# Closing a layer norm half of the tokens at a time, in a two-block float32r kernel on one core

## The chip, the core and the metric

The kernel runs on one core of a Trainium2 chip. The metric is the device time of one execution in microseconds (us). Before the change it is 2527.17 us, the median of 3 runs (2527.03 to 2527.21).

TensorE (PE) multiplies: an instruction keeps a 128x128 stationary operand, which a weight load (PEld) puts in place, and streams a moving operand of up to 512 columns past it. ScalarE (ACT), VectorE (DVE) and GpSimd (POOL) do the elementwise work, and SyncE (SP) issues the loads from memory. Each engine works through its own row of instructions in order and waits on semaphores for the others.

## What is computed

Two blocks of two layers each, on 256 tokens of 2048 features:

```python
# first block: a state-space mixer, then sparse attention, each followed by a layer norm
h = ssd_mixer(x, ...)                       # ... @ ssd_w_out: 4096 -> 2048
x = layer_norm(4**0.25 * x + h, ln_g[0], ln_b[0])
h = dsa_mixer(x, ...)                       # x @ dsa_w_in at its start, ... @ dsa_w_out at its end
x = layer_norm(4**0.25 * x + h, ln_g[1], ln_b[1])
# second block: gated MLP with token mixing, then stick-breaking attention, each behind an RMS norm
hn = rms_norm_2(h, norm_g[0]); h = h + gmlp_branch(hn, ...)      # hn @ a_w_in at its start
...
```

`layer_norm` takes mean and variance of a token over its 2048 features, so no part of its output for a token exists before the last feature of that token is there. Different tokens do not depend on each other in it.

## The kernel before, in words

All weights stream through the core once. Activations lie transposed: features on the 128 partitions, 256 tokens along the columns. `AA[:, k, 0, :]` is the leading (float32r) part of feature tile k (of 16), `AA[:, k, 1, :]` the rest, and each product is made of three float32r matmuls: leading x leading, leading weight x rest, rest of the weight x leading.

A **unit** is one load of 128x1024 weights (512 KB). SP fetches it into one of four `RAW` buffers. ACT copies it to a slot as the leading part (`e.copy`, L1038), DVE writes the rest (L1448, `RAW - leading`), and PE runs the unit's matmuls (L597). There are three slots `W0` to `W2`, and in some stretches one or two more (`WY24`, `WY28`, `Wx7`). A slot is refilled when the unit in it is done. A block is all units of one output tile: `("o1", i)` and `("o2", i)` are the output projections, in tiles of 4, 4, 4, 2, 1 and 1 feature tiles (`OUT_COLS`); `("cq", 0)` is the first block behind the first layer norm, `("v5", 0)` the first behind the second. Each has 8 units of 24 matmuls of 256 columns (`cq`) or of 12 matmuls of 512 columns (`v5`, where activations are the stationary operand and weights the moving one). `("o1", 5)` and `("o2", 5)` have 4 units of 24 matmuls of 256 columns.

The order of the work is written out by hand in `walk`: `unit(u)` lets each engine append its part of a unit, and `tick()` advances every side task, written as a generator, to its next `yield`.

At the end of a layer norm s (1 or 2), the last block's result is added to `RES` (DVE L1689), squared (ACT L1147) and summed over the features by matmuls with ones on PE (`ln_sums`). Then `ln_end` makes mean `MU` and 1/sqrt(variance) `RS` (ACT L1158 and L1160, DVE L1700 to L1707), POOL subtracts the mean from 15 feature tiles, and `norm_in` makes the first tiles of `AA` in `CHUNKS` of 1, 1, 2, 2, ... feature tiles: DVE multiplies by `RS` (L1723), ACT applies gain and bias (L1177, L1180) and copies to the leading part (L1188), DVE writes the rest (L1452). PE waits before the first matmul on each chunk:

```python
if (name == "cq" or (name, i) in (("v5", 0),)) and k in [c[0] for c in CHUNKS]:
    e.wait_ge(*on("at" + ("1" if name == "cq" else "2"), k))
```

`rms4` takes the RMS norm's sum of squares of the second layer norm's output: DVE applies gain and bias in place, POOL squares four tiles at a time and folds them, PE sums them with ones. Its result scales the output of `v5` (`ev_v5`).

Of the kernel before, what the change touches and what calls it, by code (L numbers as in the profile page):

```python
# [11 lines left out]
P = 128  # L12
T = 256
# [14 lines left out]
CHUNKS = ((0, 1), (1, 1)) + tuple((k, 2) for k in range(2, 16, 2))  # L28


class Plan:


    def __init__(self, A):
# [51 lines left out]
        self.before = {b: self.order[i - 2] if i > 1 else None for i, b in enumerate(self.order)}  # L86
        self.slots()

# [24 lines left out]
    def slots(self):  # L113
# [9 lines left out]
        for u in range(len(self.units)):  # L123
            for name, (a, z) in extra.items():
                if u == a:
                    free.append((name, None))
            alive = 3 + sum(a <= u < z for a, z in extra.values())
            free = [x for x in free if x[0] not in extra or u < extra[x[0]][1]]
            while ready < min(u + alive, len(self.units)) and free:
                self.slot[ready], self.prior[ready] = free.pop(0)  # L130
                self.turn.setdefault(u, []).append(ready)
                ready += 1
            s = self.slot[u]
            free.append((s, u))
            self.slot_end[s] = u
# [26 lines left out]
def program(nc, A, out, at, bank, counting):  # L162
# [84 lines left out]
    def region(specs):  # L247
# [16 lines left out]
        ("MU2", [P, T], F), ("RS2", [P, T], F)])  # L264
    (CK, CQ, QKB, VVB, SG, OT, KI, WT, SC, MA, TRL, PXB, PT, M8, MXB) = region([
# [8 lines left out]
        ("VS5", [P, 2, 8], F), ("VR5", [P, 2], F), ("GB5", [P, 2, 16], F)])  # L274
    (_, SQ6, GH6) = region([("keep6", [P, 16, T], F), ("SQ6", [P, 4, T], F), ("GH6", [P, 4, T], F)])
# [11 lines left out]
    SQ4, GH4 = U5, Z5  # L287
    VA = V5[:, 0, 0:5 * T].rearrange("p (a n) -> p a n", a=5)
# [5 lines left out]
    def pair_of(u):  # L294
        s = plan.slot[u]
        if s in (0, 1, 2):
            w = (W3M if units[u][0][0] == "o4" else W3)[s]
            return w[:, 0:UW], w[:, UW:2 * UW]
# [45 lines left out]
    def walk(unit, go):  # L344
# [30 lines left out]

        def later(n, *do):
# [50 lines left out]
        for i in range(1, 6):  # L427
            run(("o2", i), ("ln_block", 2, i))
        drain()
        start("ln_end", 2)  # L430
        tick()
        start("norm_in", 2)
        start("rms4", late=1)
        tick()
        for j in range(8):
            run(("v5", j), later(9 if j == 0 else 1 if j == 1 else 0, "ev_v5", j))
# [43 lines left out]
    def sync_program():  # L480
# [16 lines left out]
        def unit(u):  # L497
            for v in plan.turn.get(u, ()):
# [93 lines left out]
    def tensor_program():  # L592
# [21 lines left out]
        def unit(u):  # L614
# [3 lines left out]
            if u == us[0] and plan.before[b]:  # L618
                e.wait_ge(*on("g_read", plan.before[b]))
            e.wait_ge(*on("rest", u))  # L620
# [32 lines left out]
            for j, k in enumerate(kts):  # L653
# [6 lines left out]
                if (name == "cq" or (name, i) in (("v5", 0),)) and k in [c[0] for c in CHUNKS]:  # L660
                    e.wait_ge(*on("at" + ("1" if name == "cq" else "2"), k))
                if (name, i) == ("q7", 0) and k in [c[0] for c in OUT_COLS]:
                    e.wait_ge(*on("at3", k))
                if name in ("v5", "v7", "o4"):
                    for t in range(2):
# [12 lines left out]
            last.then_inc(*up(unit_done, "unit", u))  # L678
# [97 lines left out]
        def ln_sums(s, i):  # L776
# [14 lines left out]
            for f, v in enumerate(vals):  # L791
                ones_sum(M[:, b1, 0:T], v, i == 0 and f == 0, i == 5 and f == n - 1)
            e.wait_ge(*on("ln_sq", s, i))
            for f, v in enumerate(sqs):
                last = ones_sum(M[:, b2, 0:T], v, i == 0 and f == 0, i == 5 and f == n - 1)
            last.then_inc(*up(pe_made, "ln_m", s, i))
            if i == 5:
                ring.extend((b1, b2))
# [100 lines left out]
        def rms4():  # L899
            for i, k in enumerate(range(0, 16, 4)):  # L900
                yield
                yield
                yield
                ones_of("r5", i, SQ4[:, 0, :], ("r5_f", i), i == 3)
            yield
            yield
            yield
# [100 lines left out]
        def set8():  # L1008
# [5 lines left out]
                        ln_block=ln_block, set3=set3, ev_cq=ev_cq, ev_ms=ev_ms, index=index, attend=attend,  # L1014
# [4 lines left out]
    def scalar_program():  # L1019
        e = nc.scalar  # L1020

        def unit(u):
            for v in plan.turn.get(u, ()):
# [9 lines left out]
                elif plan.slot[v] == "y5":  # L1033
                    e.wait_ge(*on("unit", plan.blocks["o2", 5][-1]))
                elif plan.slot[v] == "x7":
# [101 lines left out]
        def ln_square(s, i):  # L1137
# [3 lines left out]
            if i == 5:  # L1141
                e.wait_ge(*on("eps"))
                e.activation(TB[:, :], eps6[:, :], ACT.Sqrt).then_inc(*up(act_made, "tb", s))
# [10 lines left out]
        def ln_end(s):  # L1154
            PV, RS = (PV2[:, :], RS2[:, :]) if s == 1 else (VA[:, 0, :], VA[:, 2, :])
            b1 = bank.get(("ln", s, 0), 0)
            e.wait_ge(*on("ln_m", s, 5))
            e.activation(PV, M[:, b1, 0:T], ACT.Square, scale=1.0 / DM).then_inc(*up(act_made, "ln_mm", s))  # L1158
            e.wait_ge(*on("read", "ln", s, 1))
# [1207 lines left out]
```

## Time and profile before

| | |
|---|---|
| median of 3 runs | 2527.17 us |
| profiled execution, its own time | 2528.34 us |
| its span from first to last instruction | 2527.1 us |
| PE busy | 2467.4 us (98%) |
| DVE, ACT, POOL busy | 64%, 49%, 5% |
| stretch from the end of ("o1", 5) to the end of ("cq", 0) | 37.99 us |
| stretch from the end of ("o2", 5) to the end of ("v5", 0) | 50.00 us |

Busy time of PE says how long an instruction was in it, its span says when the last result was there. The chain of work that ended last runs through PE for 90% of the span, so time is lost or won where PE stands still, where its clock is low, or where it has more to do.

### The profile page before, as it was taken

How to read it: one execution, taken by the hardware profiler on the slowest of the kernel's cores; microseconds unless marked ns; L12 is line 12 of the kernel's file. 1: busy time of each engine (PE TensorE's matmuls, PEld its weight loads, DVE VectorE, ACT ScalarE, POOL GpSimd, SP SyncE). 2: the span in 40 equal slices, each digit the busy share in tenths (PEclk: the TensorE clock that was granted, in tenths of full speed). 3: DMA queues.
4: the chain of work that ended last, by engine and by line, in shares of the span. 5: the costliest groups of instructions: out<-in, count | busy, mean ns of one | idle time of the engine just before them, and what ended most of it. 6: DMA issues, size and time to landing. Idle time of an engine off the chain costs nothing.

```text
span 2527.1 us, 45040 instructions
## 1 busy us (share of the span) xinstructions
PE 2467.4 (98%) x19470; PEld 2359.9 (93%) x19470; DVE 1609.6 (64%) x2120; ACT 1236.7 (49%) x1375; POOL 118.8 (5%) x96
## 2 busy tenths in 40 slices
PE   8999999999989999999979999999999999999998
PEld 8999999999979999999957889999999999899987
DVE  5778888866577776666475455665655555555556
ACT  3445665653455565643344444544544444454453
POOL 0001000100020000000050000000000000000002
PEclk9999999999999999999989999999999999999999
DMA  6766666555646555445635666666655665756645
GB/s 186 224 197 183 209 182 185 179 181 179 189 130 186 155 167 152 150 166 183 185 110 172 186 188 187 193 192 184 186 189 192 192 195 165 225 164 175 187 155 170
DMA packets 276232, 453.21 MB, mean 179 GB/s; under 512 B 18540, under 2 KB 82114, under 8 KB 274882
## 3 DMA queue, kind: packets, MB, share of 16 engines
q1 hardware_dynamic: 276033, 450.33, 59.1%
q8 instruction: 153, 2.51, 0.4%
q14 instruction: 46, 0.37, 0.0%
HBM read 445.89 MB, written 4.26 MB: 178 GB/s over the span
## 4 chain that ended last, share of the span: by engine, by line
PE 90%; DVE 5%; DMA 2%; ACT 1%; issue 1%; SPq 0%; POOL 0%; ACTq 0%; DVEq 0%; POOLq 0%
PE G L597 84%; PE M L597 6%; DVE W L1448 2%; PE M L610 1%; DMA h_scratch<-HT 1%; ACT W L1038 1%; DVE RES L1723 0%; DMA RAW<-in_b_w_in 0%; DVE AA L1452 0%; DMA CSB<-cs_scratch 0%; DMA WS<-in_a_w_s 0%; DVE WY L1448 0%; DVE BT L1487 0%; DMA XS<-in_x 0%; DMA RAW<-in_ssd_w_in 0%
## 5 line engine op out<-in xcount | busy, mean ns | idle before, releaser
L1448 DVE TENSOR_TENSOR W<-RAW,W 128x1024 fp32r<-128x1024 f32 (+1 forms) x632 | 783.6, 1242 | 589.9 <-ACT W L1038 588.2
L1038 ACT CAST W<-RAW 128x1024 fp32r<-128x1024 f32 (+1 forms) x632 | 659.1, 1048 | 738.3 <-PE G L597 708.9
L597 PE MATMUL G<-AA,W 128*128 128x256 f32 x8100 | 972.7, 279 | 18.8 <-DVE AA L1452 10.7
L597 PEld LDWEIGHTS G<-AA,W 128*128 128x128 f32 x8100 | 945.3, 189 | 27.3 <-issue 11.0
L597 PE MATMUL G<-YY,W 128*128 128x256 f32 x4608 | 534.8, 277 | 1.5 <-DVE W L1448 1.5
L597 PEld LDWEIGHTS G<-YY,W 128*128 128x128 f32 x4608 | 528.1, 188 | 4.2 <-DVE W L1448 2.4
L597 PE MATMUL G<-AA,WY 128*128 128x256 f32 x2508 | 305.8, 278 | 0.0
L597 PEld LDWEIGHTS G<-AA,WY 128*128 128x128 f32 x2508 | 293.8, 188 | 2.5 <-issue 2.2
L597 PE MATMUL G<-W,AA 128*128 128x512 f32 x864 | 216.6, 408 | 19.2 <-DVE AA L1452 15.7
L597 PEld LDWEIGHTS G<-W,AA 128*128 128x128 f32 x864 | 167.7, 195 | 62.8 <-issue 11.2
L1448 DVE TENSOR_TENSOR WY<-RAW,WY 128x1024 fp32r<-128x1024 f32 (+1 forms) x128 | 161.0, 1259 | 90.6 <-ACT WY L1038 90.5
L1038 ACT CAST WY<-RAW 128x1024 fp32r<-128x1024 f32 (+1 forms) x128 | 132.9, 1043 | 112.0 <-PE G L597 109.4
L597 PE MATMUL G<-AA,Wx 128*128 128x256 f32 x528 | 65.7, 281 | 0.0
L597 PEld LDWEIGHTS G<-AA,Wx 128*128 128x128 f32 x528 | 63.4, 192 | 0.0
L597 PE MATMUL G<-CQ,W 128*128 128x256 f32 x456 | 54.4, 278 | 0.0
L597 PEld LDWEIGHTS G<-CQ,W 128*128 128x128 f32 x456 | 52.9, 188 | 0.4 <-issue 0.3
L1268 ACT ACTIVATE PXB<-PXB,MXB 128x128 f32<-128x128 f32 x64 | 28.5, 447 | 50.2 <-DVE MXB L1906 50.1
L1038 ACT CAST Wx<-RAW 128x1024 fp32r<-128x1024 f32 x30 | 31.5, 1050 | 36.5 <-PE G L597 36.2
L1091 ACT ACTIVATE E<-E 128x1536 f32<-128x1536 f32 x16 | 23.8, 1489 | 49.7 <-DVE E L1542 49.7
L597 PE MATMUL G<-WY,AA 128*128 128x512 f32 x192 | 47.7, 396 | 0.0
L1448 DVE TENSOR_TENSOR Wx<-RAW,Wx 128x1024 fp32r<-128x1024 f32 x30 | 36.7, 1222 | 14.4 <-ACT Wx L1038 14.4
L597 PEld LDWEIGHTS G<-WY,AA 128*128 128x128 f32 x192 | 36.1, 188 | 8.9
(317 smaller groups left out, 1918.2 us busy)
## 6 DMA issues: line engine op xcount, KB each, us to landing
RAW<-in_a_w_in SPq DMA_DIRECT2D x192, 512.0 KB, 3.8
RAW<-in_ssd_w_in SPq DMA_DIRECT2D x160, 512.0 KB, 4.4
RAW<-in_b_w_in SPq DMA_DIRECT2D x128, 512.0 KB, 4.1
RAW<-in_dsa_w_in SPq DMA_DIRECT2D x72, 512.0 KB, 3.7
RAW<-in_ssd_w_out SPq DMA_DIRECT2D x64, 512.0 KB, 4.6
RAW<-in_dsa_w_out SPq DMA_DIRECT2D x64, 512.0 KB, 3.8
RAW<-in_a_w_out SPq DMA_DIRECT2D x64, 512.0 KB, 3.9
RAW<-in_b_w_out SPq DMA_DIRECT2D x32, 512.0 KB, 3.7
```

The costliest lines, as they stand in the source:

```text
L597: return e.matmul(o, l, r, start=start, stop=stop, skip_group_check=True)
L610: return e.transpose(o, i, idn)
L1038: e.copy(wh[:, 0:n], RAW[:, v % NR, 0:n]).then_inc(*up(cast_done, "cast", v))
L1091: e.activation(ev, ev, ACT.Exp).then_inc(*up(act_made, "ee", g, i))
L1268: e.activation(PX[:, a:z], PX[:, a:z], ACT.Exp, bias=MX[:, 2 + t:3 + t], accum_out=MX[:, 4 + t:5 + t]).then_inc(*up(act_made, "pe", j, h))
L1448: e.tensor_tensor(wl[:, 0:n], RAW[:, v % NR, 0:n], wh[:, 0:n].bitcast(F), ALU.subtract).then_inc(*up(rest_done, "rest", v))
```

## The change

- `("o1", 5)`, `("o2", 5)` and the first four units of `("cq", 0)` and `("v5", 0)` are done for tokens 0 to 127 and then for tokens 128 to 255. A matmul of 256 columns in `o1`, `o2` and `cq` becomes two of 128 columns. In `v5`, where the tokens are the stationary operand, the same 12 matmuls of 512 columns are only put in another order.
- `ln_close` takes the place of `ln_end`, `norm_in` and the last `ln_block`: add, square, sum, mean, root, mean subtraction, gain and both parts of `AA`, once for each half of the tokens, in five `PARTS` of 2, 2, 4, 4, 4 feature tiles.
- Four more weight slots (`WA0` to `WA3`) from the 15th unit of `("o1", 1)` to the end of `("cq", 0)`, and three (`WB0` to `WB2`) from `("o2", 1)` to the end of `("v5", 0)`.
- The squares of `rms4` move from POOL to ACT, alternate between two buffers, and `ev_v5` of block 0 starts behind the fifth unit of `("v5", 1)`.

```diff
+HALF = 128
+PARTS = ((0, 2), (2, 2), (4, 4), (8, 4), (12, 4))
+HALVED = (("o1", 5), ("cq", 0), ("o2", 5), ("v5", 0))
...
+        for b in self.order:
+            us = self.blocks[b]
+            n = 4 if b in HALVED else 0
+            self.steps += [(u, h) for h in range(2) for u in us[:n]] + [(u, None) for u in us[n:]]
...
+        for i in range(4):
+            extra[f"a{i}"] = (self.blocks["o1", 1][14], first["ms", 0])
+        for i in range(3):
+            extra[f"b{i}"] = (first["o2", 1], first["v5", 1])
...
+        def twice(b, *tasks):
+            us = plan.blocks[b]
+            for h in range(2):
+                for u in us[:4]:
+                    unit(u, h)
+                    if u == us[3] and h == 0:
+                        for t in tasks:
+                            start(*t[:-1], late=t[-1])
+                    tick()
+            for u in us[4:]:
+                unit(u)
+                tick()
...
-        for i in range(2, 6):
+        for i in range(2, 5):
             run(("o1", i), ("ln_block", 1, i))
-        drain()
-        start("ln_end", 1)
-        tick()
-        start("norm_in", 1)
-        tick()
-        run(("cq", 0))
+        twice(("o1", 5), ("ln_close", 1, 0))
+        twice(("cq", 0))
...
+        twice(("o2", 5), ("ln_close", 2, 0))
+        twice(("v5", 0), ("rms4", 2))
...
                     for f in range(width // P):
-                        o = G[:, half + f // 2, (f % 2) * T:(f % 2 + 1) * T]
+                        a, z = (0, T) if part is None else (HALF * part, HALF * part + HALF)
+                        o = G[:, half + f // 2, (f % 2) * T + a:(f % 2) * T + z]
...
-                        mm(o, h, X[:, k, 0, :], k == 0 and f % 2 == 0, False)
-                        mm(o, h, X[:, k, 1, :], False, False)
-                        last = mm(o, l, X[:, k, 0, :], False, k == nk - 1)
+                        mm(o, h, X[:, k, 0, a:z], k == 0 and first, False)
+                        mm(o, h, X[:, k, 1, a:z], False, False)
+                        last = mm(o, l, X[:, k, 0, a:z], False, k == nk - 1)
...
+            total(1)
+            normal(0, 4)
+            tails(0, 3)
+            yield
+            tails(0, 4)
+            scale(1)
+            yield
+            first_three(1)
```

On PE, at the close of the first layer norm (the one of `("o1", 5)` and `("cq", 0)`; `YY` is the projection's input, `RES_87,ones` and `SQ_89,ones` are the sums), the row before is:

```order
L597 MATMUL G<-YY,W_50 128x256 x24
L597 MATMUL M<-RES_87,ones 128x256
L597 MATMUL M<-SQ_89,ones 128x256
L597 MATMUL G<-YY,W_52 128x256 x24
L597 MATMUL M<-RES_87,ones 128x256
L597 MATMUL M<-SQ_89,ones 128x256
L597 MATMUL G<-AA,W_54 128x256 x24
L597 MATMUL G<-AA,W_50 128x256 x24
L597 MATMUL G<-AA,W_52 128x256 x24
```

and with the change, at the same place:

```order
L644 MATMUL G<-YY,WA_95 128x128 x24
L644 MATMUL G<-YY,W_50 128x128 x24
L644 MATMUL M<-RES_87,ones 128x128
L644 MATMUL M<-SQ_89,ones 128x128
L644 MATMUL G<-YY,WA_93 128x128 x24
L644 MATMUL G<-YY,WA_94 128x128 x24
L644 MATMUL G<-YY,WA_95 128x128 x24
L644 MATMUL G<-AA,WA_96 128x128 x24
L644 MATMUL M<-RES_87,ones 128x128
L644 MATMUL M<-SQ_89,ones 128x128
L644 MATMUL G<-AA,W_52 128x128 x24
L644 MATMUL G<-AA,W_54 128x128 x24
```

The sums of the first half now stand behind the first unit of the second half, with three more half units of `o1` behind them, and the sums of the second half stand behind the first half unit of `cq`. Every unit here counts 24 matmuls for 128 columns and comes twice.

On DVE, for the second half of the same layer norm, the change puts the work on the second half (L1815, L1824) between that on the first half (L1843, L1561) and the rests of the weights (L1557):

```order
L1557 TENSOR_TENSOR WA_93<-RAW,WA_93 128x1024
L1843 TENSOR_TENSOR RES_87<-RES_87,RS_92 128x4x128
L1561 TENSOR_TENSOR AA<-RES_87,AA 128x4x128
L1557 TENSOR_TENSOR WA_94<-RAW,WA_94 128x1024
L1815 TENSOR_TENSOR RES_87<-RES_87,G 128x128
L1843 TENSOR_TENSOR RES_87<-RES_87,RS_92 128x4x128
L1561 TENSOR_TENSOR AA<-RES_87,AA 128x4x128
L1557 TENSOR_TENSOR WA_95<-RAW,WA_95 128x1024
L1561 TENSOR_TENSOR AA<-RES_87,AA 128x4x128
L1824 SCALAR_TENSOR_TENSOR RS_92<-M,PV_88 128x128
```

Before, the whole row of the norm's end stood together and the weights came behind it:

```order
L1689 TENSOR_TENSOR RES_87<-RES_87,G 128x256
L1700 SCALAR_TENSOR_TENSOR RS_92<-M,PV_88 128x256
L1702 TENSOR_SCALAR MU_91<-M 128x256
L1705 TENSOR_TENSOR RES_87<-RES_87,MU_91 128x256
L1707 RECIPROCAL RS_92<-RS_92 128x256
L1723 TENSOR_TENSOR RES_87<-RES_87,RS_92 128x256
```

The addition for the second half (L1815) is the instruction for which PE's second pair of sums waits, and it stands behind two rests of weights.

## Rows read from the trace of the kernel before

**Rows 1.** The page: span, busy time of each engine.

```profile
span 2527.1 us, 45040 instructions
PE 2467.4 (98%) x19470; PEld 2359.9 (93%) x19470; DVE 1609.6 (64%) x2120; ACT 1236.7 (49%) x1375; POOL 118.8 (5%) x96
```

**Rows 2.** PE's waits, 675 to 760 us, then 1250 to 1360 us: total, times, longest.

```profile
PE G L597 <- DVE AA L1452: 10.7, 5, 6.5
PE M L597 <- DVE RES L1689: 0.5, 1, 0.5
...
PE G L597 <- DVE AA L1452: 15.7, 6, 6.5
PE G L597 <- ACT V L1315: 3.5, 1, 3.5
```

**Rows 3.** Busy time by stretch: length, each engine, granted clock, DMA share, GB/s.

```profile
697.91:735.90 37.99, 26.79 (x198) 25.50 (x199) 28.26 (x32) 22.00 (x35) 16.09 (x18) 0.87 0.32 93
...
1272.30:1322.30 50.00, 33.81 (x106) 25.23 (x106) 40.76 (x45) 23.54 (x36) 29.93 (x23) 0.80 0.32 94
1322.30:1349.33 27.03, 23.48 (x103) 18.69 (x102) 17.36 (x17) 12.40 (x14) 8.74 (x5) 1.00 0.63 176
```

**Rows 4.** Timeline, first two units of cq: start, length, engine, instruction, [idle before].

```profile
706.06 5.46 PE L597 MATMUL G<-AA,W 128*128 128x256 f32 x24 [6.50 <-DVE AA L1452]
...
712.01 3.01 PE L597 MATMUL G<-AA,W 128*128 128x256 f32 x24 [0.50 <-DVE AA L1452]
```

**Rows 5.** Timeline, five of the eight units of v5.

```profile
1280.46 5.22 PE L597 MATMUL G<-W,AA 128*128 128x512 f32 x12 [6.50 <-DVE AA L1452]
...
1288.09 4.58 PE L597 MATMUL G<-W,AA 128*128 128x512 f32 x12 [2.41 <-DVE AA L1452]
...
1295.73 4.48 PE L597 MATMUL G<-W,AA 128*128 128x512 f32 x12 [3.06 <-DVE AA L1452]
...
1303.96 3.04 PE L597 MATMUL G<-W,AA 128*128 128x512 f32 x12 [0.52 <-DVE AA L1452]
...
1313.23 5.46 PE L597 MATMUL G<-W,AA 128*128 128x512 f32 x12 [2.60 <-DVE AA L1452]
```

**Rows 6.** 256 columns by stretch, 512 columns by stretch, loads by form, narrow rows of timelines.

```profile
575.00:600.00 25.00, 25.00 (x223) 25.00 (x223) 12.58 (x11) 9.49 (x9) 0.00 (x0) 1.00 0.63 195
...
1400.00:1425.00 25.00, 25.00 (x109) 20.06 (x108) 12.26 (x13) 10.51 (x11) 0.00 (x0) 1.00 0.66 189
...
L597 PEld LDWEIGHTS G<-AA,W 128*128 128x128 f32 x8100 | 945.3, 189 | 27.3 <-issue 11.0 <-DVE W L1448 7.5 <-DVE AA L1452 6.9
...
L597 PEld LDWEIGHTS M<-E,XD 128*64 128x64 f32 x256 | 16.1, 136 | 8.3
...
1523.88 0.60 PE L597 MATMUL M<-WR,V 128*128 128x128 f32 x4
...
1523.77 0.52 PEld L597 LDWEIGHTS M<-WR,V 128*128 128x128 f32 x4
...
61.64 0.13 PEld L610 LDWEIGHTS M<-ident,SZ 64*128 64x128 f32 x1
61.70 0.14 PEld L610 LDWEIGHTS M<-ident,YT 64*128 64x128 f32 x1
```

**Rows 7.** Timeline of the first norm's end: root, mean, and one later chunk's work.

```profile
700.84 15.13 POOL L2284 TENSOR_TENSOR RES<-RES,MU 128x256 f32<-128x256 f32 x15 [150.33 <-DVE MU L1702]
701.14 1.74 DVE L1707 RECIPROCAL RS<-RS 128x256 f32<-128x256 f32 x1
...
720.71 1.09 ACT L1177 ACTIVATE RES<-RES,VC 128x256 f32<-128x256 f32 x2
720.84 1.23 DVE L1448 TENSOR_TENSOR W<-RAW,W 128x1024 fp32r<-128x1024 f32 x1 [1.98 <-ACT W L1038]
721.83 0.62 ACT L1188 CAST AA<-RES 128x512 fp32r<-128x512 f32 x1
721.98 0.68 DVE L1723 TENSOR_TENSOR RES<-RES,RS 128x512 f32<-128x512 f32 x1
```

More of the change, by code:

```diff
@@ L264, in program @@
         ("MU2", [P, T], F), ("RS2", [P, T], F)])
+    after = [s_at + 4 * (16 * T + T + 4 * T + 2 * T + T + T)]
+    WA = []
+    for i in range(4):
+        after[0] += (STILL - after[0]) % 512
+        WA.append(place(f"WA{i}", [P, 2 * UW], R, after[0]))
+        after[0] += 8 * UW
     (CK, CQ, QKB, VVB, SG, OT, KI, WT, SC, MA, TRL, PXB, PT, M8, MXB) = region([
@@ L274, in program @@
         ("VS5", [P, 2, 8], F), ("VR5", [P, 2], F), ("GB5", [P, 2, 16], F)])
+    after[0] = s_at + 4 * (16 * T + 5 * T)
+    WB = []
+    for i in range(3):
+        after[0] += (STILL - after[0]) % 512
+        WB.append(place(f"WB{i}", [P, 2 * UW], R, after[0]))
+        after[0] += 8 * UW
     (_, SQ6, GH6) = region([("keep6", [P, 16, T], F), ("SQ6", [P, 4, T], F), ("GH6", [P, 4, T], F)])
@@ L426, in walk @@
         tick()
-        for i in range(1, 6):
+        for i in range(1, 5):
             run(("o2", i), ("ln_block", 2, i))
[L429 to L436, printed above, removed]
+        twice(("o2", 5), ("ln_close", 2, 0))
+        twice(("v5", 0), ("rms4", 2))
+        run(("v5", 1), to=5)
+        start("ev_v5", 0)
+        run(("v5", 1), later(1, "ev_v5", 1), since=5)
+        for j in range(2, 8):
+            run(("v5", j), ("ev_v5", j))
         for j in range(8):
@@ L617, in unit @@
             us = plan.blocks[b]
-            if u == us[0] and plan.before[b]:
+            if u == us[0] and plan.before[b] and part != 1:
                 e.wait_ge(*on("g_read", plan.before[b]))
-            e.wait_ge(*on("rest", u))
+            if part != 1:
+                e.wait_ge(*on("rest", u))
             wh, wl = pair_of(u)
@@ L664, in unit @@
                 if name in ("v5", "v7", "o4"):
-                    for t in range(2):
+                    for t in range(2) if part is None else (part,):
                         o = G[:, half + t, 0:width]
@@ L1192, in norm_in @@
-            half(1)
-            yield
-            for c in range(2, len(CHUNKS)):
-                gain(c)
-                half(c)
-                yield
+                                         *up(act_made, "gain", s, h, c))
+                src = RES[:, k:k + n, a:z] if s == 1 else GHH[:, (5 * h + c) % 2, 0:n, :]
+                e.wait_ge(*on("gain", s, h, c))
+                e.copy(AA[:, k:k + n, 0, a:z], src).then_inc(*up(act_made, "at_h", s, h, c))
+            square(0)
+            yield
@@ L1199, in set3 @@
+            root(0)
+            yield
+            part(0, 0)
+            part(0, 1)
+            yield
+            part(0, 2)
+            yield
+            square(1)
+            part(0, 3)
+            yield
+            part(0, 4)
+            root(1)
+            yield
+            part(1, 0)
+            part(1, 1)
+            yield
+            part(1, 2)
+            yield
+            part(1, 3)
+            yield
+            part(1, 4)
+            yield
         def set3():
@@ new lines, in ln_close, with total @@
+            b = ("o1" if s == 1 else "o2", 5)
+            def total(h):
+                a, z = HALF * h, HALF * h + HALF
+                e.wait_ge(*(done(b) if h else on("half", b)))
+                if h == 0:
+                    e.wait_ge(*on("pre", s, 5))
+                e.tensor_tensor(RES[:, 15, a:z], RES[:, 15, a:z], g_of(b)[:, 512 * h:512 * h + HALF], ALU.add).then_inc(
+                    *up(dve_made, "ln_r", s, 5, h))
+                if h == 1:
+                    here(dve_made, "g_read", b)
```

317 lines of the change are left out of this document (186 added, 131 removed).

## The prediction

> **What bounds the kernel now.** I read the page first: PE is busy for 2467.4 of 2527.1 us [rows 1], so only PE's own path can give or cost much, and what DVE, ACT or POOL gain matters only where PE waits for them. The view of waits, cut to the two layer norms' ends, shows those places. At the first PE waits 10.7 us in five pieces for the chunks of AA and 0.5 us for the last addition; at the second 15.7 us in six pieces, and 3.5 us for the evaluation of v5 (with the same 0.5 us for the last addition) [rows 2]. The longest piece is 6.5 us both times: the chain from the last matmul of the projection through sums, root and first chunk, under which PE has nothing to do.
>
> Waiting is not the whole loss. The timeline has the first unit of cq at 5.46 us for 24 matmuls and the next at 3.01 [rows 4], so 2.4 us went at the lower clock, which followed the 6.5 us of idling. In v5 four units took 5.22, 4.58, 4.48 and 5.46 us where a unit at the full clock takes 3.04 [rows 5]: 7.6 us more. The granted clock over the two stretches is 0.87 and 0.80 [rows 3].
>
> What the two ends cost today is therefore 11.2 + 2.4 at the first and 19.7 + 7.6 at the second, **40.9 us**. A halving that removed all of it would give no more. The 50.00 us of the second stretch hold 8 units, of about 22 us at the rate of a 512-column matmul below.
>
> **What the change adds: the narrow matmul.** 96 matmuls of o1,5, 96 of the first four units of cq and 96 of o2,5 become 576 of 128 columns. v5 gets none more. All hangs on what one of 128 columns costs. At 256 columns 223 run in 25 us, 0.112 us each with the few float32 sums among them (a unit alone runs at 0.1137: its 24 last 3.01 us [rows 4], of which some 0.28 is the last one's latency); at 512 columns 109, 0.229 us [rows 6]. Time goes with the columns there, and the straight line would give 0.057 us at 128: two narrow ones for one wide, no cost at all. That is the lower bound.
>
> But each matmul has a weight load of its own, and halving the columns doesn't shorten the load. Loads of 128 columns last 189 ns, loads of 64 columns 136 [rows 6]: 53 ns for 64 columns, so 106 ns of a 128-column load go with its columns and the rest is a latency that overlaps. The closest row of the right width is float32: four matmuls of 128 columns last 0.60 us, and their four loads 0.52 us at 0.19 each, so that one starts each (0.52 - 0.19)/3 = 0.11 us [rows 6]. That row cannot say whether the load or the multiplication sets the pace, as float32 is also slower in the latter. Only the transposes' loads come closer together: 61.64 and 61.70, 0.06 us apart, at 0.13 to 0.14 us each [rows 6]; those of float32r last as long as the float32 ones, so I place them with these. I take **0.110 us** for a narrow float32r matmul. The upper bound: narrow float32r at the rate of narrow float32, two instructions of 0.11 each, 0.22 us. The sum at 0.110: 576 x 0.110 = 63.4 us instead of 288 x 0.1137 = 32.7, **+30.6 us** of work on the engine that is busy 98% of the time. At 0.057 it is 0, at 0.22 +94.
>
> The slope of 106 ns, above, has a rule beside it: the Trainium skill, TensorE: Matmul & The Clock Gate, section LDWEIGHTS, gives a load as its columns over 1.2, 107 ns for 128 columns; the trace's two load rows agree. By that figure alone, as an estimate, the added work would be 576 x 0.107 - 32.7 = +28.9 us instead of +30.6.
>
> **What it takes away.** I follow the order of the changed rows with durations of before. First layer norm, with t = 0 when PE has finished the first half of o1,5. The add and the square of 128 columns take about 0.3 us each; PE's sums stand behind a half unit, at 2.6; mean, variance and root with a reciprocal of about 0.9 (half of the 1.74 of 256 columns, rounded up) [rows 7] are done at 5; multiplication, two gains, copy and rest of the first part, with a weight's cast between them, at 9. The second half of o1,5 keeps PE until 4 x 2.64 = 10.6. So the 6.5 us wait is gone at the price above. Behind it:
> - The second half's addition stands on DVE behind two rests of weights at 1.23 each and the chunks at 0.68 [rows 7], some 4.5 us behind the end of o1,5. PE does one half unit of cq, 2.7, and then waits: **1.8 us**.
> - The second half's root waits on ACT behind the last part of the first half: four gains at about 0.4 and a copy at 0.62, and a cast of a weight of 1.05. From the second addition to the second half's first part of AA are 11 us; three half units of cq cover 7.9. Left: **2.5 us**.
> - The extra slots let four more weights be prepared at once, at the start of the norm's work: 4 x 1.23 = 4.9 us on DVE ahead of the first sums. I put 2.2 us of that on PE (bounds 0, if nothing waits, and 4.9).
>
> At the second layer norm o2,5 is the same, but a half unit of v5 is 6 matmuls of 512 columns, 1.4 us where that of cq is 2.6, so it covers half as much: **3.0 us** for the second addition's sums, **4.3 us** for the second half's first part. The sums of rms4 have ACT squares and POOL folds ahead of them, and PE meets the first of them early: **3.3 us**. The 3.5 us for the evaluation of v5 go, as it starts later. Gaps of 3 to 4 us stand between short units, in a place where gaps of 2.4 and 3.1 us today went with the lower clock [rows 5]: between 0 and 7 us, I take **3.5**.
>
> Left after the change: 1.8 + 2.5 + 2.2 + 3.0 + 4.3 + 3.3 + 3.5 = **20.6 us** of the 40.9. Gain 20.3. Also moved: ACT gets 32 gains of 128 columns for 15 of 256 in each norm (about 12 us for 8), and the four squares of POOL; POOL's 15 subtractions of 1.0 us [rows 7] become 8 larger ones; DVE's work stays about as long. ACT is busy 22 of 38 us in the first stretch and DVE 28 [rows 3], so these fit and are in the waits above. DMA issues stay the same in number; the queue is at a share of 0.32 in both stretches [rows 3], so the added slots find their data.
>
> **The sum.** +30.6 - 20.3 = +10.3 us. On the profiled execution's own 2528.34 us that is 2538.6, and as the runs' median lies 1.2 us under it, **2537 us**, 0.4% slower.
>
> **The rivals.**
> - *The narrow matmul costs what its columns cost* (0.057): nothing is added, but the cover is half as long, since the second half of o1,5 lasts 5.5 us. Waits at the first norm then come to 2.0 + 4.6 + 4.0 + 2.2, at the second 2.0 + 4.5 + 5.0 + 2.2, and with idling like today's some 7 of clock: 33.5. The gain is 7: 2520 us, faster. For it speaks the straight line of 256 and 512 columns; against it the length of the loads. It decides below 576 x p = 32.7 + 20, p = 0.091 us. Chance 0.12.
> - *Between the two*, where a load is partly hidden: halfway, at 0.083, the work grows by 47.8 - 32.7 = 15 us, the waits left lie halfway too, about 27, and the gain is 14: 2528, no change. Chance 0.10. The Trainium skill's page TensorE: Matmul & The Clock Gate, section Back-to-back issue gap, gives 81 ns for a sustained stream of loads and matmuls at 128 columns; no row of this trace shows it, and by it this rival would come out, 1 us lower.
> - *Narrow float32r falls to the rate of float32* (0.22): 576 x 0.218 = 125.6, +93 us; the longer units then cover all but some 5 us, so the gain is 36: 2584 us. For it speaks that the kernel has no float32r matmul under 256 columns, so no row excludes it; against it that nothing else in the trace slows with a shorter stream. Chance 0.18.
> - *The half-way work does more than I count*: at 0.110, the waits left come to 8 instead of 20.6, as the second halves' chains fall under PE's work: 2524. Chance 0.05.
>
> **How the numbers follow.** My own case, 0.110 with its waits, has 0.55; its range of 2529 to 2547 comes from waits of 12 to 30 us. A measurement of this kernel can tell 0.2%, 5 us, from no change. Faster (under 2522): most of the first rival and a little of the second, 0.13. Within 0.2% (2522 to 2532): the second, the last, and the low end of mine, 0.22. Slower: the rest of mine and the third rival, 0.65. The range that leaves no more than 2 in 10 out must take in the third rival and the second, but can leave out the first: 2523 to 2588.
>
> **What the profile after would show.** The group of 128x128 matmuls G<-YY,W and G<-AA,W, 576 of them, with 24 in 2.6 to 2.8 us between starts (the price; 1.4 would be the first rival, 5.2 the third). PE at work through the time of the 6.5 us waits, which are gone. In their place a wait of M<-RES,ones for DVE's addition behind the first half unit of cq and v5, and one before the second half's first matmul. No 3.5 us wait for ACT's V. The stretch from the start of o1,5 to the end of cq longer by 11 us (384 x 0.110 - 192 x 0.1137 = 20.4 of work, less 13.6 - 4.3 of waits), that from the start of o2,5 to the start of v5,2's matmuls shorter by 3 (10.2 of work, less 27.3 - 14.1). What would make me wrong most of all is the pace of a narrow matmul; then the clock in v5.

## The result, and the profile after

The changed kernel takes **2561.3 us** (median of 4 runs, 2557.56 to 2562.29) beside 2527.19 for the kernel before on the same chip: a ratio of 1.013, 95% interval 1.0118 to 1.0143, **slower by 34 us**. Forecast were 2537 us, +10, in a range of 2523 to 2588: the sign was right, and the loss is more than three times the size I gave it. My own case went up to 2547 only; the result lies in the range because the range had been drawn out to 2588 for the third rival. The profiled execution took 2561.48 us.

The page, first its span and engines, then the granted clock in 40 slices:

```profile
span 2560.2 us, 45695 instructions
PE 2509.7 (98%) x19766; PEld 2404.4 (94%) x19766; DVE 1603.5 (63%) x2132; ACT 1251.0 (49%) x1421; POOL 96.5 (4%) x78
...
PEclk9999999999969999999999999999999999999999
```

PE is busy 42 us longer than in [rows 1] and waits less. The single 6 in the clock's row, at about 700 to 770 us, is where the prediction had nothing.

PE's waits from 590 to 780 us, over the first norm's sums and its end (`SU` holds partial sums of `RES`), then over the second norm's end:

```profile
PE M L644 <- DVE RES L1815: 3.1, 1, 3.1
PE M L644 <- DVE SU L1760: 2.8, 1, 2.8
...
PE G L644 <- DVE AA L1561: 6.7, 1, 6.7
PE M L644 <- POOL U L2446: 4.6, 1, 4.6
PE M L644 <- DVE RES L1815: 4.3, 1, 4.3
```

Against [rows 2], waits fell from 11.2 to 3.1 us at the first norm's end and from 19.7 to 15.6 at the second. The wait of 2.8 us for SU is new; it stands earlier, in the block o1,2. Windows of the five stretches (columns as in [rows 3]): o1,5 whole; cq whole; its 168 narrow matmuls behind the wait; o2,5; v5,0:

```profile
690.61:713.31 22.70, 22.70 (x202) 22.60 (x202) 9.60 (x12) 5.78 (x13) 5.86 (x4) 1.00 0.19 61
713.31:769.00 55.69, 52.57 (x294) 52.43 (x294) 21.63 (x28) 23.87 (x48) 5.04 (x4) 0.63 0.17 50
719.91:755.70 35.79, 35.79 (x170) 35.79 (x170) 15.70 (x20) 17.22 (x36) 5.04 (x4) 0.50 0.18 55
1294.95:1317.64 22.69, 22.69 (x201) 22.59 (x201) 9.60 (x12) 7.16 (x14) 5.85 (x4) 1.00 0.20 63
1317.64:1363.80 46.16, 30.51 (x105) 23.66 (x105) 28.92 (x44) 27.59 (x51) 11.82 (x10) 0.82 0.27 80
```

The third row is the loss that I missed: PE is busy every moment of 35.79 us at a granted clock of 0.50. The timeline of PE shows what stands around it:

```profile
705.06 8.23 PE L644 MATMUL G<-YY,WA 128*128 128x128 f32 x72
713.13 2.84 PE L644 MATMUL G<-AA,WA 128*128 128x128 f32 x24
719.10 0.73 PE L644 MATMUL M<-RES,ones 128*128 128x128 f32 x2 [3.12 <-DVE RES L1815]
...
719.91 15.60 PE L644 MATMUL G<-AA,W 128*128 128x128 f32 x72
735.31 5.32 PE L644 MATMUL G<-AA,WA 128*128 128x128 f32 x24
740.43 15.56 PE L644 MATMUL G<-AA,W 128*128 128x128 f32 x72
755.79 13.20 PE L644 MATMUL G<-AA,WA 128*128 128x256 f32 x96
...
1323.43 0.80 PE L644 MATMUL M<-RES,ones 128*128 128x128 f32 x2 [4.35 <-DVE RES L1815]
...
1324.31 4.16 PE L644 MATMUL G<-W,AA 128*128 128x512 f32 x12
```

72 narrow matmuls of o1,5 take 8.07 us from start to start, 0.112 us each. The same 72 in cq, behind a wait of 3.12 us, take 15.40, 0.214 each. At the second norm (last two rows) 12 matmuls of 512 columns stand behind such a wait and take 4.16 us, where such a unit at the full clock takes 3.04 [rows 5].

Where the time went, block by block, from the end of one block to the end of the next in the two profiled executions (in us; blocks that differ by under 0.7 left out, and forecasts in the last column):

| block | before | after | difference | forecast |
|---|---|---|---|---|
| o1,2 | 47.8 | 52.4 | +4.6 | +2.2 |
| o1,5 | 11.8 | 22.7 | +10.9 | |
| cq | 38.0 | 55.7 | +17.7 | +11 with o1,5 |
| o2,1 | 46.2 | 47.3 | +1.1 | 0 |
| o2,5 | 11.8 | 22.7 | +10.9 | |
| v5,0 and v5,2 | 50.0 + 28.0 | 46.2 + 22.4 | -9.4 | -3 with o2,5 |
| z7,0 | 32.4 | 29.7 | -2.7 | 0 |
| sum | | | +33.1 | +10.3 |

+33.1 is all of the difference of the spans (2560.2 less 2527.1). The block z7,0 lies 700 us behind the change and moves by a few us in several of the runs below; I put no cause to it.

### The profile page after: what moved, and what is told of

Same layout as the page of the kernel before. It is cut to its first block, busy times and chain, and to the rows that moved or that the text cites. A ratio compares the mean times of both kernels' runs of the same rounds, so it can differ in the third digit from the quotient of the medians.

```text
span 2560.2 us, 45695 instructions
## 1 busy us (share of the span) xinstructions
PE 2509.7 (98%) x19766; PEld 2404.4 (94%) x19766; DVE 1603.5 (63%) x2132; ACT 1251.0 (49%) x1421; POOL 96.5 (4%) x78
## 4 chain that ended last, share of the span: by engine, by line
PE 90%; DVE 4%; ACT 2%; DMA 2%; issue 1%; POOL 0%; SPq 0%; ACTq 0%; DVEq 0%
PE G L644 84%; PE M L644 6%; DVE W L1557 1%; PE M L657 1%; ACT W L1117 1%; DMA h_scratch<-HT 1%; DMA RAW<-in_b_w_in 0%; ACT Z L1267 0%; DVE RES L1843 0%; DMA RAW<-in_ssd_w_out 0%; DMA RAW<-in_dsa_w_out 0%; DVE BT L1596 0%; DMA XS<-in_x 0%; DMA RAW<-in_ssd_w_in 0%; DVE HT L2324 0%
## 5 line engine op out<-in xcount | busy, mean ns | idle before, releaser
L1557 DVE TENSOR_TENSOR W<-RAW,W 128x1024 fp32r<-128x1024 f32 x581 | 717.8, 1238 | 534.9 <-ACT W L1117 532.9
L644 PE MATMUL G<-AA,W 128*128 128x256 f32 (+1 forms) x8028 | 974.8, 280 | 8.9 <-DVE W L1557 8.9
L1117 ACT CAST W<-RAW 128x1024 fp32r<-128x1024 f32 x581 | 605.5, 1047 | 643.7 <-PE G L644 613.3
L644 PE MATMUL G<-YY,W 128*128 128x256 f32 (+1 forms) x3624 | 422.4, 277 | 1.1 <-DVE W L1557 1.0
L644 PEld LDWEIGHTS G<-YY,W 128*128 128x128 f32 x3624 | 416.1, 188 | 3.4 <-DVE W L1557 1.8
L1557 DVE TENSOR_TENSOR WY<-RAW,WY 128x1024 fp32r<-128x1024 f32 (+1 forms) x128 | 160.0, 1252 | 102.1 <-ACT WY L1117 102.1
L644 PE MATMUL G<-W,AA 128*128 128x512 f32 x840 | 204.3, 399 | 6.7 <-DVE AA L1561 6.7
L644 PE MATMUL G<-YY,WB 128*128 128x256 f32 (+1 forms) x648 | 75.4, 276 | 0.0
L644 PEld LDWEIGHTS G<-YY,WB 128*128 128x128 f32 x648 | 74.2, 189 | 0.1
L644 PE MATMUL G<-YY,WA 128*128 128x256 f32 (+1 forms) x528 | 63.1, 281 | 0.0
L644 PEld LDWEIGHTS G<-YY,WA 128*128 128x128 f32 x528 | 62.1, 193 | 0.2
```

The lines of the kernel that those rows point to most:

```text
L644: return e.matmul(o, l, r, start=start, stop=stop, skip_group_check=True)
L1117: e.copy(wh[:, 0:n], RAW[:, v % NR, 0:n]).then_inc(*up(cast_done, "cast", v))
L1557: e.tensor_tensor(wl[:, 0:n], RAW[:, v % NR, 0:n], wh[:, 0:n].bitcast(F), ALU.subtract).then_inc(*up(rest_done, "rest", v))
```

## The experiments

Theory A of the loss: a narrow matmul costs 0.11 us, and a clock that stays low through narrow matmuls did the rest. Its rivals: the narrow matmul is dearer in cq for another reason (its operands, what else runs beside it); the halves' chain costs cq its time, whatever its matmuls are like; or the waits alone do. All runs are compared with the kernel before on their own chip: 2528.71 us (13 runs) for the first four, 2527.72 (15) for the next four, 2528.73 (20) for the last two.

### 1. The price by itself

The kernel before, with ten rows of matmuls behind its end that compute nothing:

```diff
+            row(300, 0, 128, 128)   # matmuls, tile of AA, stationary columns, moving columns
+            row(100, 1, 128, 256)
+            row(300, 2, 128, 128)
+            row(60, 3, 128, 64)
+            row(60, 4, 128, 192)
+            row(60, 5, 64, 128)
+            row(60, 6, 64, 256)
+            row(60, 7, 128, 512)
+            row(60, 8, 64, 64)
+            row(60, 9, 32, 128)
```

> The kernel before, with rows of matmuls on finished data put behind its last result, so its time is longer by these rows and means nothing; only their pace is read. PE stands idle for some us ahead of them, so they begin at the lower clock. Order: 300 of 128 columns, 100 of 256, 300 of 128, then 60 each of 64, 192 columns, 64 stationary columns x 128 and x 256, 128 x 512, 64 x 64, 32 x 128. Theory A (each matmul pays its weight load, and the load goes with the clock): 128 columns 0.112 us at the full clock and 0.214 at the lower; 64 columns 0.112 too, 192 columns 0.112 too; with 64 stationary columns 128 moving ones cost 0.057. Rival B (a float32r matmul has a least length of 256 moving columns whatever it loads): 64 x 128 costs 0.112 as well. Rival C (the load has a clock of its own): 0.107 to 0.112 at the lower clock too. On the clock: theory A says that the first 300 narrow ones stay at the lower clock (64 us), that the 100 wide ones bring it up, and that the next 300 keep it (34 us); the rival, that the clock rises within the first row as it does under wide ones (then 35 to 40 us).

Windows of the first row, the start and the rest of the second, the third, fourth, fifth, sixth and eighth:

```profile
2522.00:2585.00 63.00, 63.00 (x296) 63.00 (x297) 0.00 (x0) 0.00 (x0) 0.00 (x0) 0.50 0.07 29
2585.90:2590.90 5.00, 5.00 (x27) 5.00 (x27) 0.00 (x0) 0.00 (x0) 0.00 (x0) 0.55 0.00 0
2590.90:2599.60 8.70, 8.70 (x76) 8.70 (x75) 0.00 (x0) 0.00 (x0) 0.00 (x0) 1.00 0.01 2
2600.00:2633.00 33.00, 33.00 (x299) 33.00 (x297) 0.00 (x0) 0.00 (x0) 0.00 (x0) 1.00 0.00 1
2633.40:2641.20 7.80, 7.80 (x60) 7.80 (x59) 0.00 (x0) 0.00 (x0) 0.00 (x0) 0.81 0.00 0
2641.60:2651.40 9.80, 9.80 (x60) 9.80 (x61) 0.00 (x0) 0.00 (x0) 0.00 (x0) 0.65 0.01 2
2651.70:2655.00 3.30, 3.30 (x58) 3.30 (x57) 0.00 (x0) 0.00 (x0) 0.00 (x0) 1.00 0.00 0
2662.50:2675.50 13.00, 13.00 (x58) 10.54 (x57) 0.00 (x0) 0.00 (x0) 0.00 (x0) 1.00 0.00 0
```

This is one profiled execution, and only paces are read from it, each from a row's first start to its last (a window also counts matmuls that only reach into it). 300 narrow matmuls behind an idle time of 5.24 us ran at 0.50 all through, at 0.213 us each. In the row of 256 columns that followed the clock rose. The next 300 narrow ones kept it, at 0.111 each. So the same instruction cost 0.111 or 0.213 by the clock it started with, and no other reason is needed for cq. Rival C, a load with a clock of its own, falls with the 0.213.

The load is what sets 0.111. With 64 moving columns the pace was still 0.111 in the part of the row at the full clock (44 matmuls), and with 64 stationary columns under 128 moving ones it was 0.060 (seventh window), so Rival B, a least length of 256 columns, falls too. With 32 stationary columns the pace stayed at 0.060, so in these last two rows it is no longer the load that sets it.

By the Trainium skill, TensorE: Matmul & The Clock Gate, section LDWEIGHTS, a load takes its columns over 1.2, 107 ns for 128 columns. The third row agrees within 5 ns at the full clock; the first shows that at the low clock the pair of load and matmul takes twice as long.

### 2. Filler in the waits

The changed kernel with matmuls of 256 columns that compute nothing in the waits of cq and v5,0:

```diff
+        def fill(n):
+            for _ in range(n):
+                mm(M[:, b, 0:T], YY[:, 0, 0, 0:P], YY[:, 0, 0, :], True, True)
...
+                if b in (("cq", 0), ("v5", 0)) and k == 0 and part == 1:
+                    fill(34 if name == "cq" else 56)
...
+                if h == 1:
+                    fill((26, 36)[s - 1])
                 e.wait_ge(*on("ln_r", s, 5, h))
```

> The changed kernel, with matmuls of 256 columns on finished data where PE waits: 26 and 36 ahead of the second half's sums at the first and second layer norm, 34 and 56 ahead of the second half of cq and of v5. Their results are overwritten. Theory A (the wait let the clock fall, and narrow matmuls did not bring it back): the clock stays at 1.0 through cq, the 168 narrow matmuls that took 35.9 us take 19, and of the 17 us about 4 come back as a wait that the faster units uncover; in v5 some 6 us of low clock go. Together 15 to 21 us less than the changed kernel, 2541 to 2547. Rival D (the narrow matmuls of cq are slow for another reason, as they read AA while ACT and DVE write it, or the clock falls under narrow matmuls anyway): cq stays as long, and the time is 2555 to 2565.

2547.86 us (2547.35 to 2551.4), ratio 1.0081 (1.0066 to 1.0097): some 13 us under the changed kernel, 1 us over theory A's range and far from rival D's, although PE has 152 matmuls more to do. The timeline of PE in cq, and its 72 narrow matmuls:

```profile
716.10 3.29 PE L644 MATMUL M<-YY 128*128 128x256 f32 x26
...
719.98 8.23 PE L644 MATMUL G<-AA,W 128*128 128x128 f32 x72
728.05 4.19 PE L644 MATMUL M<-YY 128*128 128x256 f32 x34
732.08 2.79 PE L644 MATMUL G<-AA,WA 128*128 128x128 f32 x24
734.71 8.20 PE L644 MATMUL G<-AA,W 128*128 128x128 f32 x72
```

15.60 us became 8.23, cq fell from 55.7 to 40.3. The wait of 3.1 us was small by itself; what it cost was the clock for the 36 us behind it. The operands and what else ran beside PE were the same, so the first rival falls as well. v5,0 fell only from 46.2 to 45.6: there the fillers kept the clock at 1.00 up to the wait for POOL, and the time went to fillers and waits instead (5.5 us for POOL, 2.1 for chunks of `AA`).

### 3. Narrow matmuls without halves

The kernel before, each matmul of o1,5, o2,5 and four units of cq as two of 128 columns, one after the other, in the old order:

```diff
+                        if b in (("o1", 5), ("o2", 5)) or (b == ("cq", 0) and u in us[:4]):
+                            for z in (0, P):
+                                mm(o[:, z:z + P], h, X[:, k, 0, z:z + P], ...)
+                                mm(o[:, z:z + P], h, X[:, k, 1, z:z + P], False, False)
+                                last = mm(o[:, z:z + P], l, X[:, k, 0, z:z + P], ...)
```

> The kernel before with one part of the change alone: each matmul of o1,5, o2,5 and of the first four units of cq is made as two of 128 columns right behind each other; order, chains and slots stay. Theory A: 10.8 us more for each of o1,5 and o2,5; in cq the 6.5 us wait lets the clock fall, the narrow matmuls keep it low, and the four units take 41 us of work instead of 14: +24 to +27 there, less what chunk waits they cover (3). In all 2527 + 43 to 47 = 2570 to 2574. Rival D (low clock rises under narrow matmuls as under wide ones): +10.8 in cq too, less 3 of waits: 2557.

2573.85 us (2572.29 to 2575.26), ratio 1.0179 (1.0162 to 1.0196), inside theory A's 2570 to 2574 and far over rival D's 2557. o1,5 and o2,5 took 22.2 each, cq 64.0. One row of the timeline and its window; the row takes together the 192 narrow matmuls (41.0 us) and 48 of 256 columns behind them:

```profile
717.57 49.14 PE L597 MATMUL G<-AA,W 128*128 128x128 f32 x240 [6.50 <-DVE AA L1458]
```

```profile
717.57:766.60 49.03, 49.03 (x240) 48.94 (x240) 17.00 (x19) 15.89 (x25) 8.45 (x9) 0.53 0.16 46
```

Without any change of order, 45 us are lost (47 in the profiled executions, of which 21 on the two projections' blocks and 26 in cq). Of the later waits for chunks of cq only one of 1.0 us is left; matmuls at half the pace cover the others. So the split alone costs 11 us more than the whole change. The rest of the change gives that back: in the profiles 8.3 us in cq, 2.6 in v5,0 and 6.7 in v5,2, less 4.6 in o1,2 for the early slots. The gain in v5,2 has little to do with the halves, as experiments 8 and 9 show.

### 4. Filler in the kernel before

54 such matmuls behind the last sums of each norm, in the 6.5 us waits of [rows 2].

```diff
             last.then_inc(*up(pe_made, "ln_m", s, i))
             if i == 5:
+                fill(54)
```

> The kernel before, with 54 matmuls of 256 columns on finished data in the 6.5 us wait of both layer norms, behind the last sums. Nothing else changes. Theory A (the wait costs clock beyond itself): the first unit of cq takes 3.0 us and not 5.46, those of v5 3.04 and not 5.22, 4.58, 4.48, at least until the waits of 2.4 and 3.1 us; 5 to 10 us less, 2517 to 2522. If the low clock's work is hidden under the chunk waits anyway: no gain in cq's chunks, 2525 to 2527.

2526.75 us (2521.82 to 2529.33), ratio 0.9992 (0.9982 to 1.0001): no difference from the kernel before. The windows of cq and v5,0:

```profile
697.90:735.30 37.40, 31.33 (x252) 29.80 (x252) 28.65 (x32) 22.10 (x35) 16.62 (x18) 1.00 0.33 96
1272.30:1322.10 49.80, 38.44 (x160) 30.15 (x161) 40.49 (x45) 23.71 (x37) 30.32 (x23) 0.86 0.33 94
```

The clock of cq rose from 0.87 to 1.00, and the block went from 38.0 to 37.4, not by the 2.4 us that I had called lost; PE now waits for the later chunks instead. My theory's 2517 to 2522 missed, its alternative held. In v5,0 the clock rose only to 0.86, so that run says less on its 7.6 us.

### 5. The other operand stationary

The changed kernel with cq multiplied as v5 is, so that its half units keep 512 moving columns:

```diff
-                if name in ("v5", "v7", "o4"):
+                if name in ("v5", "v7", "o4", "cq"):
```

> The changed kernel, with cq multiplied the other way round, as v5 is: the tokens stand in TensorE's array and a row of 512 weights moves, so that a half unit of cq is 12 matmuls of 512 columns instead of 24 of 128. The halves of the norm and their chain stay as they are. cq's result lands in another layout than the rest of the kernel reads it in (the later steps compute on it as it is), only the time is meant. Theory A (what the change costs at the first norm is the narrow matmul and the clock, not the halving): the 96 wide matmuls of cq that became 192 narrow ones cost 10.2 us of the full clock, and about 17 us because narrow matmuls ran at a granted clock of 0.50 behind the wait of 3.1 us. With 512 columns the first goes, and the clock rises sooner, as it does in v5: cq 35 to 42 us where the changed kernel has 55.7, the whole at 2533 to 2541 us. Rival (the chain of the halves costs cq its time, whatever its matmuls look like): short half units cover less of the chain, the waits in cq grow from 3 to over 10 us, the whole stays above 2550.

2542.41 us (2541.03 to 2544.63), ratio 1.0057 (1.0043 to 1.007), some 19 under the changed kernel and a little over the range that A gave (2533 to 2541). The second half's wait in the timeline of PE:

```profile
718.47 0.79 PE L644 MATMUL M<-RES,ones 128*128 128x128 f32 x2 [4.35 <-DVE RES L1815]
...
730.63 2.93 PE L644 MATMUL G<-WA,AA 128*128 128x512 f32 x6 [5.70 <-DVE AA L1561]
```

cq took 37.3, as A said (35 to 42). But its waits were 10.1 us, as the rival said, though the whole stayed well under the rival's 2550. Both were at work: with wide matmuls there is no added work and a low clock for some units only (0.77 and 0.69 in the windows behind the two waits), and the shorter half units cover 7 us less of the chain. The block is then as long as before the change (38.0): **in cq the halving gains 0.7 us even where its matmuls cost nothing more**, and 10.9 are still paid in o1,5.

### 6. The slots later

```diff
-            extra[f"a{i}"] = (self.blocks["o1", 1][14], first["ms", 0])
+            extra[f"a{i}"] = (first["o1", 4], first["ms", 0])
```

> The changed kernel, with the four extra weight slots of the first norm open from o1,4 on instead of from the 15th unit of o1,1, so that DVE doesn't prepare four weights ahead of the norm's first sums. Theory A (the 4.6 us that o1,2 grew by, 47.8 to 52.4, are these four preparations ahead of the first sums, with a PE wait of 2.8 us on DVE's SU and some clock behind it): o1,2 at 48 to 49 us, the whole 3 to 5 us under the changed kernel, 2556 to 2558. Rival (o1,2 grew by something else of the new order): o1,2 stays at 52, the whole at 2561. Should the slots be missed later on, a wait for the data of WA appears in o1,5 or cq.

o1,2 went back to 47.8 and its wait for SU is gone. So the 4.6 us come from the early slots, that is the four rests of weights ahead of the norm's first work. The whole doesn't show it: 2559.82 us (2558.78 to 2560.41), 1.5 under the changed kernel where 3 to 5 were expected, and the intervals of the two ratios overlap (1.0111 to 1.0138 beside 1.0118 to 1.0143). The profiled spans differ by 1.3: o1,2 gave 4.6 and cq 0.9, while k7,1, 1400 us further on and untouched, took 2.6 more and z7,0 and the first block 1 each. What moved them stays open.

### 7. The projections' last blocks whole

On top of experiment 2: o1,5 and o2,5 are done 256 columns wide, then 66 filler matmuls, then the first half unit of cq or v5.

```diff
+            whole = b in (("o1", 5), ("o2", 5))
+            if whole:
+                if part == 1:
+                    return
+                part = None
...
+                if b in (("cq", 0), ("v5", 0)) and k == 0 and part == 0:
+                    fill(66)
```

> The changed kernel with filler matmuls in the waits (2547.9 us), but the four units of o1,5 and of o2,5 are multiplied whole, 256 columns wide, and then the chain of the first half starts: 192 narrow matmuls fewer in each... that is 384 narrow ones become 192 wide. The 192 half-unit matmuls no longer stand over the chain, 66 filler matmuls stand there in their place, before the first half unit of cq and of v5. Theory A (the second half of o1,5, 10.9 us of narrow matmuls, ends exactly as late as the first half's chain, and costs 10.9 us more than half of the wide block did save): the block loses 10.9 us and the wait ahead of cq and of v5 gains about as much, less what the two wide blocks' start saves; the whole stays within 4 us of 2548. Rival (the narrow cover is dearer than what it covers): 5 us or more faster, under 2543. Second rival (its cover is worth more): over 2553.

2544.09 us (2541.16 to 2545.67), ratio 1.0065 (1.0049 to 1.008): 3.8 under experiment 2, within the 4 us of theory A, near its edge; 2.8 when each is taken against the kernel before on its own chip. The timeline of PE across the place:

```profile
701.20 0.49 PE L644 MATMUL M<-SQ,ones 128*128 128x128 f32 x2
701.44 8.05 PE L644 MATMUL M<-YY 128*128 128x256 f32 x66
709.34 2.79 PE L644 MATMUL G<-AA,WA 128*128 128x128 f32 x24
```

Each projection block lost its 10.9 us (22.7 to 11.8), and what follows grew by 9.3 (cq 40.3 to 49.6) and 8.9 (v5,0 45.6 to 54.5). From its sums on, the first half's chain needs 8 us at most (no wait stands behind the fillers), and 66 matmuls that compute nothing cover it as well as the second half of o1,5 did. The reason can be read in the starts: whole, the block of 96 matmuls and the sums among them ends 11.8 us behind its start; halved, its *first half* ends there (690.4 to 702.1 in the changed kernel), as 96 narrow matmuls take as long as 96 wide ones. The chain of the first half doesn't begin any sooner, and the second half is 10.9 us of added work over a chain of 8.

### 8. The squares on ACT alone

The kernel before, with the squares of `rms4` on ACT (one buffer, as before), their sums two units apart, and `ev_v5` of block 0 three units sooner:

```diff
+                e.activation(flat(SQ4[:, :, :]), flat(RES4[:, k:k + 4, :]), ACT.Square)
...
-            run(("v5", j), later(9 if j == 0 else ...
+            run(("v5", j), later(6 if j == 0 else ...
```

> The kernel before, with one part of the change alone: the squares of the last norm's sums are made on ACT instead of POOL, their steps stand two units apart instead of three, and the evaluation of v5,0 stands three units earlier. No matmul is halved. Theory A (the wait of 3.5 us for V, which the changed kernel has lost, went because of this part and not because of the halves): the wait goes, v5,2 falls from 28.0 to 22 to 24 us, the whole is 3 to 5 us under the kernel before, about 2523 to 2525. Rival (it went because the halves leave more units between): the wait comes back as one for POOL's folds or for the sums, the whole within 1 us of before or over it.

2532.58 us (2531.55 to 2534.38), ratio 1.0018 (1.0009 to 1.0027): 5 us slower, where theory A had 2523 to 2525. v5,2 fell from 28.0 to 22.4, as expected: the wait for V is gone without halves. But v5,0 grew by 10.1 us, which had not been foreseen. The row of ACT shows how:

```profile
1310.65 0.62 ACT L1187 CAST AA<-Z 128x512 fp32r<-128x512 f32 x1
1318.95 1.06 ACT L1302 ACTIVATE U<-RES 128x1024 f32<-128x1024 f32 x1 [7.68 <-PE M L597]
```

The square waits until PE has summed the one before, and the copies for the next chunks of `AA`, for which PE itself waits, stand behind it on ACT. In the changed kernel the squares alternate between two buffers.

### 9 and 10. The scale's turn one unit sooner

In the kernel before, the reciprocal of the last norm's scale is done 4.6 us before PE turns it (1340.80 and 1345.40). Only this was changed, then the same with experiment 4's fillers:

```diff
             yield
             yield
-            yield
             turn_scale("r5")
...
-            run(("v5", j), later(9 if j == 0 else ...
+            run(("v5", j), later(8 if j == 0 else ...
```

> The kernel before, with only this changed: the turn of the last norm's scale (two small matmuls on TensorE) stands one unit earlier, and the evaluation of v5,0 on ACT as well. No matmul is halved and the squares stay on POOL. Theory A (the 3.5 us for which TensorE waited for V come from where these steps stand in the order, since the reciprocal was done 4.5 us before TensorE turned it; the halving isn't needed to lose this wait): 3 us of the 3.5 go and no chunk of AA comes later, the whole 2 to 5 us under the kernel before, about 2523 to 2525. Rival (the wait is set by the sums of the norm and moves to another place): the whole within 1 us of before.

> The same with the filler matmuls in the two waits of 6.5 us as well. Theory A: the fillers bring 0 to 1 us more, as the chunks of AA set the pace behind the wait and not the clock; 2522 to 2525. Rival (with the later wait gone the clock stays up and the fillers pay after all): 3 us or more under the version without them.

2524.31 us (2519.18 to 2527.6), ratio **0.9983** (0.9974 to 0.9991), and with fillers 2521.16 (2518.41 to 2523.94), ratio **0.9971** (0.9961 to 0.998). The wait at v5,2, where it was 3.5 us:

```profile
1342.64 0.38 PE L610 MATMUL M<-ident,RSK 128*128 128x128 f32 x2
...
1346.57 5.63 PE L597 MATMUL G<-W,AA 128*128 128x512 f32 x23 [0.75 <-ACT V L1314]
```

v5,2 fell to 23.4, as expected. These two beat both kernels. The fillers brought 3.1 us here, where theory A gave them 0 to 1 and the rival 3 or more, and 2.0 in experiment 4. But where they stand they gave little: in the profiled executions cq fell by 0.7 and v5,0 grew by 0.1, and 2.0 of the 2.8 us lie in z7,0, which also moves by itself. The intervals of the two ratios overlap, too. I claim no more than that the fillers cost nothing.

## Why the prediction was right and wrong

**The range.** It held by luck. The 2588 at its top stands for a narrow float32r matmul that costs 0.22 us at any clock, and that is false: it costs 0.111 at the full clock. The narrow matmuls of cq did take 0.214, near that price, but for a reason that none of the rivals had. My own case, with its 2529 to 2547, missed by 14 us.

**The narrow matmul (+30.6).** Right. I took 0.110 us; it is 0.112 in o1,5 and o2,5, 0.111 by itself. o1,5 and o2,5 grew by 10.9 each where 10.2 was forecast. The first two rivals (0.057, 0.083) and the third (0.22) fall at the full clock. The 81 ns that the second rival had beside it, from TensorE: Matmul & The Clock Gate, section Back-to-back issue gap, in the Trainium skill, isn't seen in 300 back-to-back pairs of a 128-column load and a 128-column matmul of float32r.

**The clock ("between 0 and 7 us, I take 3.5").** This is the step that failed. I placed the clock at v5 alone, where "gaps of 3 to 4 us stand between short units", and gave the wait of 1.8 us in cq no clock at all. That wait was 3.1 us. Behind it 168 narrow matmuls took 35.9 us instead of 168 x 0.112 = 18.8, +17.1, and the 96 wide ones of cq then 13.0 instead of 10.9, +2.1: **19 us** from a term that I hadn't written down. Of the miss of 23 us between +10.3 and +33.1 it is the bulk. Experiment 2 gives 15.4 of it back with nothing but filler; the rest went to its 34 fillers, 4 us that stand where the slow matmuls had covered the chain of the second half. In v5 the matmuls of v5,0 were slower by some 6 us at the low clock (46.2 less 96 x 0.229 of matmuls, 15.6 of waits and about 2 of sums), inside the bound but over 3.5. That this was a loss of its own isn't shown: experiment 2 took 4 of the 6 away, and the block gave 0.6.

**"What the two ends cost today ... 40.9 us".** Over-counted, but not seen in the result's size. The 2.4 of clock in cq was no loss of its own: experiment 4 took it away and got 0.6. Where the chunks of `AA` come at their own pace, a slow matmul between them is covered.

**Left after the change.** Second half's addition in cq: 1.8 forecast, 3.1 measured. Second half's first part in cq: 2.5 against none, since the narrow matmuls at half pace cover it. The slots: 2.2 against 4.6, near the upper bound of 4.9, shown by experiment 6; 2.8 of them are the wait for SU, and the clock was low for 3.4 us behind it. At v5: 3.0 against 4.3, 4.3 against 6.7, 3.3 against 4.6. Those of the second norm were too small by 1.3 to 2.4. The order of the waits was right at every place but one, their sum without clock 17.1 against 23.3.

**The 3.5 us for V.** Gone, as I said, and 1.7 of clock behind it went too (36 matmuls took 10.21 us behind the wait, and 8.56 the next time). Experiments 8 and 9 show that it came from the place of a few steps in the order, and that the halves have no part in it.

**What the profile was to show.** From the start of o1,5 to the end of cq: +11 forecast, +28.6 measured. From the start of o2,5 to v5,2's matmuls: -3 forecast, +3.5 measured, 6.5 more. The waits are larger by 5.0, o2,5's matmuls by 0.7 and the slow matmuls of v5,0 by some 2.4, together 8.1; where the 1.6 between the two went I can't say.

## What to carry to other kernels

Before halving a tile to start a chain sooner, ask when the first half ends. If the weight load sets a matmul's pace, half the moving columns take the whole time; then the chain starts where it did and the second half is added work. With the halved dimension on the stationary side the matmul stays wide and nothing is added; in experiment 5 that took away the price, but the halved norm still gave cq only 0.7 us.

A wait has two prices, its length and the clock behind it, and the second depends on what follows: in v5, the 12 matmuls of 512 columns behind a wait of 4.35 us took 4.16 us instead of 3.04, while 168 matmuls of 128 columns stayed at 0.50 to their end after one of 3.1. And low-clock time that lies between waits for a slower chain may be no loss: experiment 4 raised the clock in cq from 0.87 to 1.00 and gained 0.6 us there. Last, a wait that goes with a large change may hang on a few steps' place in the order: here moving them by one unit gave 4 us, with nothing halved.

## What the runs showed that I had not expected

- The granted clock did not rise in 63 us of back-to-back narrow matmuls (296 in the window, all at 0.50), and did not fall in 33 us of the same when they began at 1.00.
- It also fell with no idle time at all: in the row of 60 matmuls of 64 moving columns, behind 300 at 1.00, the window shows 0.81, and the 60 of 192 columns that followed were at 0.65 on average. The next row stood at 1.00 again. Why it fell there, and not in the 300 before, no run here shows.
- At a granted clock of 0.50 a matmul bound by its load slows about as much as one of 512 columns: 0.213 against 0.111 us here, and 5.46 against 3.04 us for the 12 matmuls of the last unit of [rows 5], through which the clock of the kernel before was 0.50.
